# The even mixer in one block: scan groups behind its tiles of values, attention steps behind its tiles of gates

## What is computed

```python
def even_mixer(x, mix_norm, w_in, ...):
    proj = rms_norm_2(x, mix_norm) @ w_in                     # 1024 -> 4608 (+ 32 rates)
    q, k, v, z, xbc, dt_raw = jnp.split(proj, EVEN_SPLITS, axis=-1)
    # q and k are normed per head (8 heads)
    na_out = neighbourhood_attention(q, k, v, na_rel_bias)
    xbc = jax.nn.silu(centred_depthwise_conv(xbc, conv_w, conv_b))
    xs, bm, cm = jnp.split(xbc, ...)                           # 16 heads, 4 groups of B and C
    y = y_fwd + y_bwd + D_skip[:, None] * xs                   # two chunked SSD scans
    ssd_out = gated_group_rms_norm(y, z, out_norm)             # (y * silu(z)), normed per group
    return jnp.concatenate([na_out, ssd_out], axis=-1) @ w_out
```

## Time and profile before

| what | value |
| --- | --- |
| time, median of 3 runs (lowest to highest) | 3037.36 us (3036.32 to 3039.28) |
| the profiled execution's own time | 3039.76 us |
| its span | 3037.9 us |
| PE busy | 2808.3 us (92%) |
| DVE busy | 1577.2 us (52%) |
| ACT busy | 1021.0 us (34%) |
| POOL busy | 715.2 us (24%) |
| mean granted clock of PE | 0.949 |

### The profile page before, as it was taken

One profiled execution on the slowest core, in us unless ns is written; L12 is line 12 of the kernel. 1 busy time (PEld: TensorE's weight loads), 2 busy tenths in 40 slices (PEclk: granted clock), 3 DMA queues, 4 the chain that ended last, 5 costly groups with the idle time before them and its releaser, 6 DMA issues. The chain is left out here.

```text
span 3037.9 us, 37787 instructions
## 1 busy us (share of the span) xinstructions
PE 2808.3 (92%) x13754; PEld 2234.4 (74%) x13754; DVE 1577.2 (52%) x1987; ACT 1021.0 (34%) x1789; POOL 715.2 (24%) x665
## 2 busy tenths in 40 slices
PE   6799999799999999999999885799999888999999
PEld 4678888556788878888678672588888655788887
DVE  3367773464633467774574565554433437654432
ACT  3323332224333334332253433432222226522221
POOL 0031111322631441112100252631111103421100
PEclk9999999899988999999999986899999888999999
DMA  3213223311100023323222101132223210022233
GB/s 126 71 56 97 97 94 90 102 56 45 60 8 19 1 70 97 97 88 96 83 90 90 49 1 37 24 101 97 96 92 96 90 56 1 31 95 97 97 90 104
DMA packets 79530, 218.94 MB, mean 72 GB/s; under 512 B 21805, under 2 KB 21933, under 8 KB 79022
## 3 DMA queue, kind: packets, MB, share of 16 engines
q1 hardware_dynamic: 78974, 213.94, 22.8%
q10 hardware_dynamic: 432, 3.32, 0.3%
HBM read 215.14 MB, written 2.10 MB: 72 GB/s over the span
## 5 line engine op out<-in xcount | busy, mean ns | idle before, releaser
L307 PE MATMUL psum<-rounded,high_r 128*128 128x512 f32 x3040 | 1201.0, 395 | 57.1 <-DVE rounded L272 26.3
L309 PE MATMUL psum<-rounded,high_r 128*128 128x512 f32 x3040 | 1192.0, 392 | 0.0
L311 PE MATMUL psum<-rounded,ring_low 128*128 128x512 f32 x3040 | 1191.0, 392 | 0.0
L327 ACT ACTIVATE high_r<-ring 128x1024 fp32r<-128x1024 f32 (+2 forms) x432 | 420.3, 973 | 1455.6 <-PE psum L311 1432.6
L332 DVE TENSOR_TENSOR ring_low<-ring,high_r 128x1024 fp32r<-128x1024 f32 (+2 forms) x430 | 520.9, 1212 | 601.0 <-ACT high_r L327 599.7
L307 PEld LDWEIGHTS psum<-rounded,high_r 128*128 128x128 f32 x3040 | 575.7, 189 | 205.6 <-issue 55.5
L311 PEld LDWEIGHTS psum<-rounded,ring_low 128*128 128x128 f32 x3040 | 576.0, 189 | 120.9
L309 PEld LDWEIGHTS psum<-rounded,high_r 128*128 128x128 f32 x3040 | 576.2, 190 | 118.6 <-issue 1.0
L764 DVE TENSOR_TENSOR arena<-psum,inverse 128x512 f32<-128x512 f32 x176 | 121.5, 691 | 314.2 <-PE psum L311 314.1
L620 POOL CAST rounded<-rows 128x512 f32 (+1 forms) x88 | 53.8, 612 | 785.5 <-DVE rows L769 785.5
L1973 POOL TENSOR_SCALAR arena<-arena,small 128x512 f32<-128x512 f32 x64 | 99.6, 1563 | 190.1 <-DVE small L1942 189.0
(11 more groups left out here) (358 smaller groups left out, 2910.6 us busy)
## 6 DMA issues: line engine op xcount, KB each, us to landing
ring<-in_up SPq DMA_DIRECT2D x176, 512.0 KB, 3.3
ring<-in_down SPq DMA_DIRECT2D x64, 384.0 KB, 3.1
ring<-in_down SPq DMA_DIRECT2D x64, 320.0 KB, 2.9
ring<-in_even_in SPq DMA_DIRECT2D x36, 512.0 KB, 3.5
ring<-in_sgu_in SPq DMA_DIRECT2D x16, 512.0 KB, 3.3
ring<-in_even_out SPq DMA_DIRECT2D x16, 384.0 KB, 3.1
ring<-in_qkv SPq DMA_DIRECT2D x12, 512.0 KB, 3.5
ring<-in_sgu_out SPq DMA_DIRECT2D x8, 512.0 KB, 3.3
```

The costliest lines, as they stand in the source:

```text
L307: nc.tensor.matmul(psum[:, m, :], high_r[:, r % HIGHS, blk], x_high, start=(k0 + k == 0), stop=False)
L309: nc.tensor.matmul(psum[:, m, :], high_r[:, r % HIGHS, blk], x_low, start=False, stop=False)
L311: mm = nc.tensor.matmul(psum[:, m, :], ring_low[:, r % R, blk], x_high, start=False, stop=end)
L327: nc.scalar.activation(high_r[:, r % HIGHS, 0:nk * P], ring[:, r % R, 0:nk * P], ACT.Copy).then_inc(unit_high, 1)
```

## The change

The even mixer becomes one block (`even`, in `joined()`, with `feed_forward(2)` inside), without a barrier between its stages. The tiles come in the order q and k (0 to 7), conv (8 to 23, CONV to VALUES), v (24 to 27, VALUES to GATES), z (28 to 35, GATES to TILES). Behind each v tile PE runs 8 scan units; behind z tile 28 it runs step 0, and behind each further one two attention steps (and turns y back, or gathers squares of gated tiles). Steps 15 to 19 and the norm over groups follow the last tile. ACT and DVE run the same units and steps in `beside(n)`, DVE two units behind PE's cut. All v and z tiles use bank 7 alone; a tile waits until the one before it is scaled. Q and k norms move to n = 5 to 20, with two banks (6 and 7) for the spreads. `keep` (the skip term included) moves from ACT to DVE, `bring` has one bank (6) where it had two, and the separate gate, transposes with skip, `to_tokens`, `split_tiles` and norm blocks are gone; their instructions stand between the steps or behind them. The final norm of the residual moves to n = 2 to 9. SP loads the bias windows between ring units 30 to 35, each pair behind a wait. The weights of `even_out` are split ahead of its block.

In the diff, ACT's and POOL's halves, which follow PE's order, and the deleted functions (`ssd`, `neighbourhood`, shown above as the kernel before) are left out.

```diff
-        SPLIT_LATE = ("sgu_in", "rwkv_o", "even_out")
+        SPLIT_LATE = ("sgu_in", "rwkv_o")
...
                     first = isinstance(g, int) and g == 0
-                    if k0 == 0:
+                    if bank_of:
+                        m = bank_of(g * st.tiles + m)
+                    elif k0 == 0:
...
+            CONV, VALUES, GATES, TILES = 8, 24, 28, 36
...
+                i = n - VALUES
...
+                return range(max(2 * (n - GATES) - 1, 0), 2 * (n - GATES) + 1)
...
+                    for n in range(R, TILES):
+                        sp.wait_ge(unit_done, st.first + n - R + 1)
+                        load_unit(sp, st, n // R, n % R)
+                        if n == 30:
+                            sp.wait_ge(b_turned, 4)
+                            window_of(0)
+                            window_of(1)
...
+                        if n == 35:
+                            sp.wait_ge(na_biased, 16)
+                            window_of(6)
+                            window_of(7)
...
+                    for r in range(R):
+                        sp.wait_ge(unit_done, following.first - R + r + 1)
+                        load_unit(sp, following, 0, r)
...
+                    def bank_of(n):
+                        if n < VALUES:
+                            wait(pe, scaled, n - 3)
+                            return n % 4
+                        if n == VALUES:
+                            pe.wait_ge(qk_done, KD)
+                        pe.wait_ge(scaled, n)
...
+                    def spread_qk(i):
...
+                        if i >= 2:
+                            pe.wait_ge(qk_done, i - 1)
+                        nc.tensor.matmul(psum[:, 6 + i % 2, :], Heads.spread(i), rows[strip(i % 4), 0, :], start=True, stop=True).then_inc(qk_spread, 1)
...
+                    def bring(n):
+                        grp, j = n // 4, n % 4
+                        pe.wait_ge(state_kept, 2 * (grp + 1))
+                        if n:
+                            pe.wait_ge(brought_scaled, n)
...
+                    def scan_unit(u):
+                        for ahead in (u + 3, u + 4):
+                            if u % 2 == 0 and ahead < UNITS:
+                                spread(ahead)
+                        if u % 8 == 4:
+                            if u > 8:
+                                bring(4 * (u // 8 - 1) + 3)
+                            states(u // 8)
+                        inside(u)
+                        if u % 8 == 5 and u + 8 < UNITS:
+                            products_bc(u // 8 + 1)
...
+                    def step(i):
+                        if i < STEPS:
+                            j, qt = divmod(i, 4)
+                            wait(pe, na_biased, 2 * i)
...
+                            u = i - 3
+                            pe.wait_ge(na_normed, 2 * u + 2)
+                            if u:
+                                pe.wait_ge(na_turned_kept, u)
+                            else:
...
+                    def turn_y(j):
+                        if j == 0:
+                            pe.wait_ge(added, HEADS)
+                        else:
+                            pe.wait_ge(gated, j)
...
+                    def spread_gated(i):
+                        if i == 0:
+                            pe.wait_ge(gate_inverted, 1)
+                            pe.wait_ge(scaled, TILES)
+                        if i >= 2:
+                            pe.wait_ge(gate_normed, i - 1)
+                        nc.tensor.matmul(psum[:, (5, 7)[i % 2], :], Groups.spread(i), rows[strip(Groups.strip_of(i)), 0, :],
...
+                        if 12 <= n < 20:
+                            turn_xs(n - 12)
+                        if 16 <= n < 20:
+                            spread_qk(2 * n - 32)
+                            spread_qk(2 * n - 31)
+                        if n == VALUES - 1:
+                            spread(0)
+                            spread(1)
+                            products_bc(0)
+                            spread(2)
+                        if VALUES <= n < GATES:
+                            for u in range(8 * (n - VALUES), 8 * (n - VALUES) + 8):
+                                scan_unit(u)
+                        if n == GATES - 1:
+                            bring(12)
...
+                        if n >= GATES:
+                            for k, i in enumerate(steps_behind(n)):
+                                if n % 2 == 0 and n > GATES:
+                                    turn_y(n - GATES - 2 + k)
+                                step(i)
+                            if n % 2 and n > GATES + 2:
+                                gather_gated(n - GATES - 3)
+                                gather_gated(n - GATES - 2)
+                    products(pe, name, x_parts, scaled, after_unit=beside, bank_of=bank_of)
+                    for i in LAST_STEPS:
+                        if i < 17:
+                            turn_y(i - 9)
+                        step(i)
+                        if i == 17:
+                            gather_gated(6)
+                            gather_gated(7)
+                    for i in range(KD):
+                        spread_gated(i)
...
-                        if n >= REST:
-                            act.wait_ge(scaled, n + 1)
-                            nc.scalar.activation(home(n), home(n), ACT.Silu).then_inc(silu_done, 1)
+                        if n > GATES and n % 2:
+                            for z in (n - 1, n):
+                                act.wait_ge(scaled, z + 1)
+                                nc.scalar.activation(home(z), home(z), ACT.Silu).then_inc(silu_done, 1)
...
+                    def step(i):
+                        if i >= 8 and i % 4 == 0:
+                            out_of(i // 4 - 2)
+                        if 3 <= i < STEPS + 3:
+                            u = i - 3
+                            act.wait_ge(na_turned, u + 1)
+                            if u >= 2:
+                                act.wait_ge(pv_done, u - 1)
+                            else:
+                                act.wait_ge(v_kept, PAIRS)
+                            nc.scalar.activation(pt[u % 2], psum[:, 2:4, :], ACT.Copy).then_inc(na_turned_kept, 1)
+                        if i < STEPS:
...
+                        if n == GATES:
+                            dve.wait_ge(inside_done, UNITS)
+                        nc.vector.tensor_tensor(zs(n) if CONV <= n < VALUES else home(n), psum[:, m if n < VALUES else 7, :], inverse[:, 0, :],
+                                                ALU.mult).then_inc(scaled, 1)
...
+                    def keep(h):
+                        dve.wait_ge(inside_done, 2 * h + 2)
+                        y = xt[:, :, h * HD:(h + 1) * HD]
+                        nc.vector.scalar_tensor_tensor(out=y, in0=y, scalar=col("ssd_D", h),
+                                                       in1=psum[:, 2 + h % 2, 0:4 * HD].rearrange("p (c f) -> p c f", c=NCH),
+                                                       op0=ALU.mult, op1=ALU.add).then_inc(y_kept, 1)
+                    def scan_unit(u):
+                        if u + 2 < UNITS and u % 2 == 0:
+                            argue(u + 2)
+                        dve.wait_ge(expd, u + 1)
+                        if u % 8 == 0:
+                            dve.wait_ge(bc_kept, 2 * (u // 8) + 2)
+                        nc.vector.tensor_tensor(work[:, u % 4, :], work[:, u % 4, :], masked(u // 8, u % 2), ALU.mult).then_inc(weighted, 1)
+                        first = 4 * (u // 8 - 1)
+                        if u >= 8 and u % 8 in (2, 3):
+                            bring(first + u % 8 - 2)
+                        if u % 8 == 4:
+                            if u > 8:
+                                bring(first + 2)
+                                bring(first + 3)
+                            carry(u // 8)
+                        if u % 8 == 6 and u + 8 < UNITS:
+                            mask(u // 8 + 1)
+                        if u % 2 and u >= 3:
+                            keep(u // 2 - 1)
...
-                        if n == 30:
+                        if n == 15:
                             dve.wait_ge(qk_rooted, 1)
                             nc.vector.reciprocal(rows[:, 0, :], rows[:, 2, :]).then_inc(qk_inverted, 1)
-                        if n in (32, 34):
-                            for i in range(2 * n - 64, 2 * n - 60):
+                        if 17 <= n < 21:
+                            for i in (2 * n - 34, 2 * n - 33):
                                 x = arena[:, Q + i, :]
                                 dve.wait_ge(qk_spread, i + 1)
-                                nc.vector.scalar_tensor_tensor(out=x, in0=x, scalar=col("na_qk", i), in1=psum[:, 4 + i % 4, :],
```

(31 more changed lines are left out.)

802 lines of the change are left out of this document (437 added, 365 removed).

## The result

| kernel | median us (lowest to highest, runs) | ratio to the kernel before, 95% interval |
| --- | --- | --- |
| before | 3036.75 (3027.59 to 3039.28, 6) | |
| after | 3049.19 (3048.2 to 3049.82, 6) | 1.0044 [1.0031, 1.0057] |

The change makes the kernel 0.44% slower, 12.4 us. The forecast was 3012 us, so 37 us are missing, and the time is above the range. Executions of the kernel before spread more than those of the kernel after: of 61 later ones 46 took 3027 to 3042 us and 15 took 3045 to 3052, so that the 12.4 us are a difference of medians. The profiled execution of the kernel after took 3048.2 us, its span is 3046.4 us. The even mixer goes from its first product at 1487.85 to the first product of `even_out` at 1968.26, 480.4 us where it was 469.0. (It starts 2.1 us earlier than before; the stages ahead of it are shared by both kernels.)

The account below looks back on a forecast made before the run. PE bounds the projection, no engine the 244 us behind it. Pieces 180.0 + 127 + 106 + 30.4 make 443.4 us for 469.0, a gain of 25.6: 3012 us, own range 3002 to 3023, wider range 2992 to 3042.

Parts of the forecast that it names:

- A: Tiles 0 to 23 with the q/k norms: 180.0 us after, 159.7 before, with new waits behind tiles 16 to 19.
- the clock's part: Lower PE clock behind a wait: 2.5 us each behind tiles 17 to 19, none at n = 16.
- B: Value tiles and scan: 127 us after, 118 before; start 21, then groups of 22, 29, 29 and 26.
- what DVE can do while PE runs the tile, 3.2 us: Scan groups: one `keep`, arguments and two weighings on DVE lie beside PE's tile, taking 3.2 us off a group.
- C: Gate tiles and attention: 106 us; six tiles of 12.9 us, tile 28 12, tile 29 16.5; PE bounds.
- D: Behind tile 35, last attention steps and norm: output projection starts after 30.4 us.
- Rival 3: Attention keeps 4.4 us a step with the tile on top (15.0 a tile), groups at their upper end: 3031 us; 15%.
- Rival 5: SP's waits starve the ring and tiles follow the steps, 5 us for each of four pairs: about 3037 us; 6%.
- Rival 4: Lower granted clock in the gate tiles and attention, half of the work in it, +46 us: 3058 us; 11%.

Follow-up runs that it names:

- e1: The kernel after, with each pair of q/k spreads two tiles behind the one before it (n = 16, 18, 20, 22): 3027.37 us.
- e7: The kernel after, plus idle matmuls on PE in the seven longest waits of the first two stretches: 3031.64 us.
- e5: The kernel after, with all four tiles of values one behind the other and all 32 scan units behind the last: 3041.84 us.
- e11: The kernel after, without DVE's 16 operations that take a head's result out of its bank and add the skip term: 3049.23 us.
- e12: e9, but the products that bring the carried states in write banks 6 and 7 by turns: 3002.28 us.
- e9: The kernel after, with q/k spreads two tiles apart, two output banks, first values copied behind tile 28, and the scan behind all value tiles: 3005.54 us.
- e2: The kernel after, with the scan's cut for a tile of values moved from the group's border to behind unit 4, beside DVE's carry: 3049.43 us.
- e3: The kernel after, with the products with the values in banks 4 and 5 by turns of the pair: 3038.46 us.
- e10: e9, plus idle matmuls on PE in its longest scan waits and ahead of the first products of B and C: 2999.50 us.

## Why the prediction was wrong

**A, the q/k norms: right in mechanism, 4.9 us short.** Three waits behind tiles 17 to 19 and a smaller one at 16 came where they were forecast (4.92 for 5.3 us, 1.62 for 2.2); the wait at n = 5 went. What was mis-sized is the lower clock: I took 2.5 us behind each from the one gap of 2.80 us, and behind the gaps of 4.92 us it is 4.0 (2.73 + 8.18 for 1.13 + 5.73), 2.9 and 4.0, so the three stalls cost 25.7 and not 23.4 us; behind the 1.62 us of tile 16, where I had left the clock's part out, tile 17 takes 7.35 us for 5.73. That is 3.9 of the 4.9 us. e1 shows the 20 us, e7 the clock's share.

**B, the scan: the step "what DVE can do while PE runs the tile, 3.2 us" failed.** Start 21.1, as forecast. The groups with their tiles were to take 106 us and took 114.5; the two whole ones 30.7 for 29, the last 30.95 (1777.46 to 1808.41) for 26. For the tile my terms were 5.4 + 1.9 - 3.2 = 4.1 us, the 3.2 for DVE's work hidden beside it; e5 shows that nothing is hidden and the tile adds 5.9 us. These 1.8 us are all of the miss in each of the two whole groups (30.7 for 28.9). The rest of the sum, 23.0 + 1.8 for the moved `keep`, gives the 24.8 us of e5's group by luck: e11 shows that `keep` costs nothing, and e12 that `bring` with one bank, which I had put at 0, costs about that much (units 8 to 24 take 50.5 us in e9 and 46.8 in e12, 1.9 a group). The wrong view behind both is that DVE's sum of work sets the group. It is a chain through PE, and PE's speed in it depends on its waits: e2 moved a wait of 3.6 us away and got the same length back at a clock of 0.83.

More than half of B's miss is the last group, 5.0 us. I gave it 3 us less than the others, for the products of a next group that it hasn't; but there PE waits 5.50 us for the weighing behind the carry and not 3.56. In the carry two multiplications on DVE take 4.49 us for the 1.57 of the group before, while POOL adds the first bias window, which the change put there:

```profile
1795.17 4.49 DVE L2604 TENSOR_TENSOR arena<-arena,rows 128x256 f32<-128x256 f32 x2 [1.07 <-ACT arena L2427]
```
```profile
1795.08 4.31 POOL L2804 TENSOR_TENSOR arena<-arena,const 128x896 f32<-128x896 f32 x2
```

In e12 the window comes later in the carry, at 1767.65, and the later two multiplications are the slow ones (4.35 us from 1767.86 on, the earlier two 1.50). No run has the window elsewhere, so what it costs in all isn't measured.

**C, the gate tiles: one wait overlooked, and PE's own work taken too small.** 17.7 us. The wait for the last pair's output (L2282 behind L2652) is in none of my sums: a product with the values can't begin a new pair before ACT has copied and DVE subtracted the old one, in one bank. It hits steps 8 and 12 here and step 16 in D; with the clock 11.7 us (e3) in C and D together. The rest is PE's: in e3, where no such wait is left, tiles 30 to 35 are (1922.91 - 1839.34)/6, some 13.9 us apart and not 12.9. A tile is 5.7 us with what stands at its ends and not 5.4, the two gathers 1.90 and not 0.8, the turning of y 1.3:

```profile
1866.04 1.90 PE L2297 MATMUL psum<-rows,const 128*32 128x512 f32 x4
```

The two gathers of a tile write the same strip of 32 rows and follow each other. Before, neighbours wrote different strips, and all eight took 5.24 us, mostly at the lower level, for 7.62 now at the upper. The parts of a step stayed what they were the earlier trace rows; 0.56 us of waiting between the two was forecast as 0.5. Tile 28 took 13.6 (12 forecast), tile 29 17.25 (16.5).

**D: the order right, 5.8 us short.** POOL ends 11.1 us in (11.2 forecast). The copy ends at 16.6 and not 13.3, because PE stood 2.71 us for the output bank and ran on at the lower clock; Sqrt and reciprocal follow in the forecast 2.0 and 3.4. The spreads take 14.2 us and not 11.6, at the lower level, as nearly all of the sixteen records were before, when they had four banks and took 9.78 us:

```profile
1954.11 14.23 PE L2306 MATMUL psum<-rows,const 32*128 32x512 f32 x16 [4.23 <-DVE rows L2764]
```

**The rivals.** Rival 3 (15.0 us a gate tile) gave the measured pitch, 15.5, for the wrong reason: POOL, with 58.6 of 123.7 us busy, is never late (PE waits for it nowhere). Rival 5 (the ring starved by SP's waits) has nothing for it: no product of a tile waits for its weights. Rival 4, the one on the slower side, placed the clock's loss in the gate tiles, where the clock is 0.91; its mechanism did weigh, but in A and B (PE busy at the lower level for 29 and 39 us, in the projection and the scan of before for 9 and 31) and not in C and D (37 us, 42 before): some 12 us for the 24 us more, and 17.6 us of the time come back when seven waits are filled. I had weighed the clock wait by wait, for the waits that I had seen, with one price, and made the range from durations alone. The tiles themselves are not slowed by standing in the scan: the one at 1746.74 takes 5.57 us at a granted clock of 1.00 (0.84 was the scan's mean before), and a group has 0.86 without its tile (e5) and 0.89 with it.

The Trainium skill ("TensorE: Matmul & The Clock Gate", What's actually happening) says that the throttled state is the default and activity releases it. The runs agree: with idle matmuls in the waits the group's granted clock was 1.00 for 0.89. The same page (A second HAM failure mode: psum-queue depth-cycling) describes another kernel, in bf16, whose PE stands still for moments between groups of matmuls, so often that its level goes up and down; e2 looks alike, with 10.7 us at the lower level behind 1.25 and 0.77 us of waiting. Of "ScalarE: Activation LUTs" (What ACT_TABLE_LOAD costs) no drain shows in the kernel after either: the Sqrt starts 1.30 us after the start of its table load, and the load 0.02 us behind the end of the copy before it.

```profile
1948.74 1.28 ACT L2530 ACT_TABLE_LOAD   x1
1950.04 0.63 ACT L2530 ACTIVATE rows<-rows 128x512 f32<-128x512 f32 x1
```

## What to carry to other kernels

Before dense matmul tiles are moved in between stages full of short waits, price each wait as itself plus the lower clock behind it (here 2.9 to 4.0 us behind 4.9), and count the tiles' own time: where the chain passes through PE itself, as in this scan, a tile hid nothing. Where a bank is freed by an engine that has its regular work for the tile first, leave a whole tile between the two uses, or a second bank; that alone was worth 20 and 11 us. When banks are saved, look whether small matmuls on different strips then still run side by side. Waits that can't be removed can be filled with matmuls that nobody reads.

## What the hardware showed that I had not expected

- The clock can fall without a long gap: in e2 PE waited 1.25 and 0.77 us (until 1746.91 and 1749.40), and the matmuls from 1749.40 on were at the lower level for 10.7 us. That a gap under 2.8 us costs no clock, with which I had set the clock's part at n = 16 to nothing, is wrong: tile 17 took 7.35 us for 5.73 behind 1.62 us.
- The same wait doesn't always cost the same: behind three waits of 4.92 us the lower level lasted 7.9, 5.4 and 7.4 us, behind the one of 2.80 us 5.0.
- Two multiplications of DVE that take 1.57 us in one group take 4.49 us in another, while POOL adds a window of 128x896 twice, 4.31 us. It is so in the traces of after, e5, e7, e9, e10 and e12; that one causes the other is read from the times, no run was made for it.
- Spreads from different strips of 32 rows into different banks overlap: four in 1.14 us, where two take 1.13.
- Filled waits keep the level: 17.6 us in seven places (e7), 6.0 in five (e10).
- What stays open: why in e10 the clock still falls at 1752.10, in the last group, behind waits of no more than 0.6 us, while in the group before it stays at 1.00. No run here tells that apart.
